# A Trainium2 decoder layer: column halves with query tiles 0,3 and 1,2, inverse sums as repeated stationaries, and separate semaphores for two reloads

## What is computed

```python
def one_block(args):            # a block of 128 queries
    q_blk, i = args
    s = jnp.einsum('bqhd,bkhd->bhqk', q_blk, k).astype(jnp.float32) * scale
    s = jnp.where(kpos[None, :] <= qpos[:, None], s, -jnp.inf)
    p = jax.nn.softmax(s, axis=-1).astype(v.dtype)
    return jnp.einsum('bhqk,bkhd->bqhd', p, v)
...
mix = jnp.concatenate([y_rwkv, y_mla], axis=-1) @ w_out[l]
x = layer_norm(ALPHA * x + mix, ln1_g[l], ln1_b[l])
f = jnp.square(jax.nn.relu(x @ w_ffn1[l])) @ w_ffn2[l]
x = layer_norm(ALPHA * x + f, ln2_g[l], ln2_b[l])
```

## Time and profile before

| | |
|---|---|
| time, median of 3 runs | 1356.23 us (1355.48 to 1357.2) |
| the profiled execution's own time | 1353.33 us |
| its span in the profile | 1351.5 us |
| granted TensorE clock, mean | 0.998 |
| busy of the span: PE, PEld | 97%, 79% |
| busy of the span: DVE, ACT, POOL | 70%, 35%, 37% |
| chain that ended last, PE's share | 49% |

### The profile page before, as it was taken

The page is one execution under the profiler, slowest core; times in us unless marked ns, Lnnn a source line. Parts: engine busy times, 40 slices in busy tenths (PEclk is TensorE's granted clock), DMA queues, the critical chain, the costliest instruction groups (busy, mean ns, idle before and its releaser), DMA issues.

```text
span 1351.5 us, 23894 instructions
## 1 busy us (share of the span) xinstructions
PE 1315.0 (97%) x9900; PEld 1071.2 (79%) x9900; DVE 945.5 (70%) x1110; ACT 474.8 (35%) x796; POOL 497.0 (37%) x323
## 2 busy tenths in 40 slices
PE   7999999999999989989999999999999999999997
PEld 6877677877776789986688878888888888888886
DVE  3657975257777634439677988877777787669877
ACT  3143643146555433334104522212222444333330
POOL 0000112001876210002084778766774354444030
PEclk9999999999999999999999999999999999999999
DMA  5111444779639952224222345444436986666562
GB/s 225 62 48 32 141 157 156 184 169 292 183 101 288 221 127 53 59 64 140 87 101 94 117 137 198 142 147 164 156 125 226 356 288 219 190 198 200 190 205 106
DMA packets 147372, 214.50 MB, mean 159 GB/s; under 512 B 79960, under 2 KB 86240, under 8 KB 146624
## 3 DMA queue, kind: packets, MB, share of 16 engines
q1 hardware_dynamic: 146976, 211.92, 49.3%
q10 hardware_dynamic: 288, 1.05, 0.2%
HBM read 137.89 MB, written 66.39 MB: 151 GB/s over the span
## 4 chain that ended last, share of the span: by engine, by line
PE 49%; DVE 3%; POOL 1%; issue 1%; ACT 1%; DVEq 0%; POOLq 0%; ACTq 0%
PE banks L2523 23%; PE banks L2410 18%; PE banks L2326 5%; PE banks L2398 2%; POOL tile_h L3083 1%; PE banks L2371 1%; DVE wout_lo L2736 0%; POOL tile_s L3083 0%; DVE y_all L2756 0%; DVE first_relu L2870 0%; PE banks L2352 0%; DVE gn_scale L2747 0%; PE banks L156 0%; PE banks L2337 0%; DVE yr_full L2762 0%
## 5 line engine op out<-in xcount | busy, mean ns | idle before, releaser
L2523 PE MATMUL banks<-stage_b_hi,stage_a_hi 128*128 128x512 f32 x448 | 174.3, 389 | 0.0
L2523 PE MATMUL banks<-stage_b_lo,stage_a_hi 128*128 128x512 f32 x448 | 174.3, 389 | 0.0
L2523 PE MATMUL banks<-stage_b_hi,stage_a_lo 128*128 128x512 f32 x448 | 174.3, 389 | 0.0
L2898 DVE TENSOR_TENSOR stage_a_lo<-stage_a_raw,stage_a_hi 128x1024 fp32r<-128x1024 f32 x56 | 97.7, 1745 | 35.2 <-ACT stage_a_hi L2665 35.2
L2665 ACT ACTIVATE stage_a_hi<-stage_a_raw 128x1024 fp32r<-128x1024 f32 x56 | 59.4, 1061 | 120.9 <-DMA stage_b_raw<-in_w_ffn 98.4
L2523 PEld LDWEIGHTS banks<-stage_b_lo,stage_a_hi 128*128 128x128 f32 x448 | 84.1, 188 | 17.6
L2523 PEld LDWEIGHTS banks<-stage_b_hi,stage_a_hi 128*128 128x128 f32 x448 | 84.1, 188 | 17.4
L2523 PEld LDWEIGHTS banks<-stage_b_hi,stage_a_lo 128*128 128x128 f32 x448 | 84.1, 188 | 17.3
L852 POOL TENSOR_TENSOR hT<-hT,rate 128x1024 f32<-128x1024 f32 x4 | 13.5, 3370 | 210.1 <-DVE kk_tile L773 210.1
L428 PE MATMUL banks<-xT_hi,win_hi 128*128 128x512 f32 x288 | 90.6, 396 | 0.0
L428 PE MATMUL banks<-xT_lo,win_hi 128*128 128x512 f32 x288 | 88.8, 389 | 0.0
(11 more groups left out here) (423 smaller groups left out, 3590.1 us busy)
## 6 DMA issues: line engine op xcount, KB each, us to landing
stage_b_raw<-in_w_ffn SPq DMA_DIRECT2D x50, 512.0 KB, 5.0
stage_a_raw<-hid_s SPq DMA_DIRECT2D x32, 512.0 KB, 4.0
w_landed<-in_w_ffn SPq DMA_DIRECT2D x30, 512.0 KB, 4.7
hid_s<-tile_s SPq DMA_DIRECT2D x60, 256.0 KB, 4.4
stage_a_raw<-hid_h SPq DMA_DIRECT2D x24, 512.0 KB, 4.0
hid_h<-tile_h SPq DMA_DIRECT2D x42, 256.0 KB, 2.0
win_raw<-in_w_in SPq DMA_DIRECT2D x20, 512.0 KB, 3.6
x_tok<-in_x SPq DMA_DIRECT2D x8, 512.0 KB, 7.6
```

The source lines that it names most:

```text
L2523: last = nc.tensor.matmul(ps[:, bank, :], s[a][:, j, tok], s[b][:, j, :], start=p == 0 and j == 0 and n == 0, stop=p == NP - 1 and j == 1 ...
L2898: V.tensor_tensor(s["a_lo"][:], s["a_raw"][:], s["a_hi"][:].bitcast(F32), ALU.subtract).then_inc(lo2, 1)
```

## The change

- `k.halves_of = ((0, 3), (1, 2))`: in each group, column half 0 takes the first and the last query tile, half 1 the two in the middle. As long as both of a half's tiles need a key tile, one matmul of 256 columns reads them with a stride; after that, one of 128 columns serves the farther tile.
- The inverse sums are no longer spread over a diagonal. Each column of inverse sums, repeated 64 times by its access pattern, is the stationary operand, and the identity is the moving one: four matmuls of 128 columns for each group in place of two of 256. DVE's two products with the identity are gone, with the wait before them; the addition of the two units' sums becomes a reduction (one input), and the reciprocal waits for the same group's inverse of the head before.
- `k.quarters` addresses two query tiles that aren't neighbours, so y leaves in pieces of 128 columns (512 bytes) in place of 256 (1 KB): eight DMAs of 64 KB for each head in place of four of 128 KB. `y_moved` counts 128 a head.
- `cum` and `beta` get semaphores of their own. ACT's first decays wait for `cum` alone. DVE waits for the three first reloads at the end of the stage, and SP for everything as before.

```diff
--- before.py
+++ after.py
@@ -878,7 +878,7 @@
     late_t = (mem.at("late_probs_t_03", 134, [P, 4, HALF]), mem.at("late_probs_t_45", 197, [P, 2, HALF]),
               mem.at("late_probs_t_67", 201, [P, 2, HALF // 2]))
     early_t = (mem.at("early_probs_t_01", 76, [P, 2, HALF]), mem.at("early_probs_t_23", 80, [P, 2, HALF // 2]))
-    inverse_diag = [mem.at(f"inverse_sums_diagonal{c}", kb, [P, 2, P]) for c, kb in enumerate((110, 190))]
+    inverse = mem.at("inverse_sums", 3.75, [P, TT])
     w_nope = (k.w_nope_raw, mem.at("w_nope_hi", 197, [P, QLT, NH, HD], F32R),
               mem.at("w_nope_lo", 106, [P, QLT, NH, HD], F32R))
     w_last = mem.at("w_nope_last_hi", 76, [P, QLT, 2, HD], F32R)
@@ -913,7 +913,6 @@
     tops = mem.at("row_max_parts", 3.25, [P, 2, TT])
     sums = mem.at("row_sums", 3.5, [P, 2, TT])
     total = mem.at("row_sums_added", 3.625, [P, 4])
-    inverse = mem.at("inverse_sums", 3.75, [P, TT])
     zeros = mem.at("zeros", 112, [P, HALF])
     dram = lambda name, shape: nc.dram_tensor(name, shape, F32, kind="Internal").ap()
     nope_d, rope_d, key_d = ([dram(f"{n}_d{j}", [NH * rows, S]) for j in range(2)]
@@ -926,7 +925,9 @@
     flat = lambda pair, rows=slice(0, P): ps[rows, pair[0]:pair[0] + 2, :].rearrange("p b n -> p (b n)")
     lo64, hi64, pe32, sw32 = slice(0, 64), slice(64, 128), slice(64, 96), slice(96, 128)
     halves = [slice(b * HALF, (b + 1) * HALF) for b in range(2)]
-    k.quarters = lambda x, rows, tile, c: x[rows, tile, :].rearrange("p (a c j) -> p a c j", a=2, c=2)[:, :, c, :]
+    k.halves_of = ((0, 3), (1, 2))
+    k.quarters = lambda x, rows, tile, c: x[rows, tile, :].rearrange("p (a t q) -> p a t q", a=2, t=4)\
+        [:, :, k.halves_of[c][0]:k.halves_of[c][1] + 1:k.halves_of[c][1] - k.halves_of[c][0], :]
 
     SOLVE_FROM = (SB - 2, 20, 15, 10, 0)
     LATE = {0: ("nope", 3), 1: ("key", 2), 3: ("key", 3)}
@@ -1008,7 +1009,8 @@
             "b_values_taken", "b_late_hi", "b_late_lo", "b_last_hi")
         stage_out = sems(nc, ctx, "b_stage_out0", "b_stage_out1")
         set_in = sems(nc, ctx, "b_set_in0", "b_set_in1", "b_set_in2")
-        bias_ready, first_exps, head0_in = sems(nc, ctx, "b_bias_ready", "b_first_exps", "b_head0_in")
+        bias_ready, first_exps, head0_in, cum_in = sems(nc, ctx, "b_bias_ready", "b_first_exps", "b_head0_in", "b_cum_in")
+        beta_in, = sems(nc, ctx, "b_beta_in")
         s_done, exp_done, t_done = sems(nc, ctx, "b_s_done", "b_exp_done", "b_t_done")
         evicted = sems(nc, ctx, "b_evicted_dve", "b_evicted_act")
         inverse_ready = sems(nc, ctx, "b_inverse_late", "b_inverse_early")
@@ -1095,8 +1097,10 @@
                         sp.dma_start(blocks(k.inv_d, c), solved[c][:]).then_inc(x_out, 16)
                 if h >= 5:
                     sp.wait_ge(s_done, NU * (h + 1))
-                    dst, src = ((k.cum_all, k.cum_d), (k.beta_all, k.beta_d))[h - 5]
-                    sp.dma_start(dst[:], src).then_inc(reloaded, 16)
+                    if h == 5:
+                        sp.dma_start(k.cum_all[:], k.cum_d).then_inc(cum_in, 16)
+                    else:
+                        sp.dma_start(k.beta_all[:], k.beta_d).then_inc(beta_in, 16)
                 if h == 6:
                     sp.wait_ge(x_out, 32 * NB)
                     sp.dma_start(k.first_v[:], k.v_d[:, :, 0:CH]).then_inc(first_in, 16)
@@ -1112,11 +1116,14 @@
                 sp.wait_ge(y_split, 4 * h + 4)
                 for c in range(2):
                     for dst, src in ((ym_hi, k.att_hi), (ym_lo, k.att_lo)):
-                        sp.dma_start(k.quarters(dst, rows, h // 2, c).bitcast(F32),
-                                     src[64 * c:64 * c + 64, :].rearrange("p (a j) -> p a j", a=2).bitcast(F32))\
-                            .then_inc(y_moved, 16)
-            sp.wait_ge(y_moved, 64 * (NH - 1))
-            sp.wait_ge(reloaded, 16 * 5)
+                        for a in range(2):
+                            part = src[64 * c:64 * c + 64, 2 * P * a:2 * P * (a + 1)].rearrange("p (t q) -> p t q", t=2)
+                            sp.dma_start(k.quarters(dst, rows, h // 2, c)[:, a, :, :].bitcast(F32), part.bitcast(F32))\
+                                .then_inc(y_moved, 16)
+            sp.wait_ge(y_moved, 128 * (NH - 1))
+            sp.wait_ge(reloaded, 16 * 3)
+            sp.wait_ge(cum_in, 16)
+            sp.wait_ge(beta_in, 16)
             sp.wait_ge(small_in, 16 * 5)
             sp.wait_ge(first_in, 16 * 7)
 
@@ -1237,28 +1244,35 @@
                         left(LATE[h])
                     else:
                         pe.wait_ge(y_read[g], h)
+                base = (4, 0)[g]
                 for kt in kts:
-                    for c in range(2):
-                        q0 = (4, 0)[g] + 2 * c
-                        if kt > q0 + 1:
-                            continue
-                        if g == LATER:
-                            src, at = ((late_t[0][:, kt, :], 4) if kt < 4 else (late_t[1][:, kt - 4, :], 4) if kt < 6
-                                       else (late_t[2][:, kt - 6, :], 6))
-                        else:
-                            src, at = (early_t[0][:, kt, :], 0) if kt < 2 else (early_t[1][:, kt - 2, :], 2)
-                        lo = max(kt, q0) * P
-                        last = mm(ps[64 * c:64 * c + 64, BANK_Y + g, lo - q0 * P:2 * P], v_all[:, kt, h, :],
-                                  src[:, lo - at * P:(q0 + 2 - at) * P], start=kt == 0, stop=kt == q0 + 1)
+                    if g == LATER:
+                        src, at = ((late_t[0][:, kt, :], 4) if kt < 4 else (late_t[1][:, kt - 4, :], 4) if kt < 6
+                                   else (late_t[2][:, kt - 6, :], 6))
+                    else:
+                        src, at = (early_t[0][:, kt, :], 0) if kt < 2 else (early_t[1][:, kt - 2, :], 2)
+                    for c, (near, far) in enumerate(k.halves_of):
+                        near, far = base + near - at, base + far - at
+                        out = ps[64 * c:64 * c + 64, BANK_Y + g, 0:2 * P]
+                        if kt <= near + at:
+                            last = mm(out.rearrange("p (t q) -> p t q", t=2), v_all[:, kt, h, :],
+                                      src.rearrange("p (t q) -> p t q", q=P)[:, near:far + 1:far - near, :],
+                                      start=kt == 0, stop=False)
+                        elif kt <= far + at:
+                            last = mm(out[:, P:2 * P], v_all[:, kt, h, :], src[:, far * P:(far + 1) * P],
+                                      start=False, stop=kt == far + at)
                 if kts[-1] == (7, 3)[g]:
                     last.then_inc(pv_done[g], 1)
 
             def inverse_out(h, g):
 
                 pe.wait_ge(inverse_ready[g], h + 1)
-                for c in range(2):
-                    last = mm(ps[64 * c:64 * c + 64, BANK_Y + g, 2 * P:4 * P], ones[:, 0:HD],
-                              inverse_diag[c][:].rearrange("p j q -> p (j q)"), start=True, stop=True)
+                of = (4, 0)[g]
+                for j in range(2):
+                    for c in range(2):
+                        last = mm(ps[64 * c:64 * c + 64, BANK_Y + g, (2 + j) * P:(3 + j) * P],
+                                  inverse[:, of + k.halves_of[c][j]:of + k.halves_of[c][j] + 1].to_broadcast([P, HD]),
+                                  ident[:], start=True, stop=True)
                 last.then_inc(y_done[g], 1)
 
             for name in FRONT[EARLY:11]:
@@ -1386,7 +1400,7 @@
                     if late_step(h, i - 1) is not None:
                         stage_late(h, late_step(h, i - 1))
                     if h == NH - 1 and i == 6:
-                        act.wait_ge(reloaded, 16 * 5)
+                        act.wait_ge(cum_in, 16)
                         act.wait_ge(x_out, 32 * NB)
                         A_(k.first_decay[:], k.cum_all[:, :, 0:CH], ACT.Exp, scale=-EXP_M05)
                         A_(k.first_undecay[:], k.cum_all[:, :, 0:CH], ACT.Exp, scale=EXP_M05).then_inc(first_exps, 1)
@@ -1462,18 +1476,12 @@
                 dve.wait_ge(exp_done, NU * h + (8, 12)[g])
                 row_sums = sums[:, 0, of]
                 if g == LATER:
-                    step.mark(V.tensor_tensor(total[:], sums[:, 0, of], sums[:, 1, of], ALU.add))
+                    step.mark(V.reduce_sum(total[:], sums[:, :, of].rearrange("p m q -> p q m"), AX_X))
                     step.wait()
                     row_sums = total[:]
-                step.mark(V.reciprocal(inverse[:, of], row_sums))
-                step.wait()
-                if h or g == EARLIER:
-                    dve.wait_ge(y_done[1 - g], h + g)
-                for c in range(2):
-                    pair = inverse[:, of][:, 2 * c:2 * c + 2].rearrange("p (j o) -> p j o", o=1).to_broadcast([P, 2, P])
-                    square = ident[:].rearrange("p (o q) -> p o q", o=1).to_broadcast([P, 2, P])
```

(10 more changed lines are left out.)

## The result

The changed kernel took 1360.5 us (median of 13 runs, 1356.8 to 1366.1) where the kernel before took 1355.4 on the same chip: ratio 1.0041, 95% interval 1.0027 to 1.0055. The likeliest case of the forecast, no change at 1356.7, did not come. The time lies inside the range, nearest to rival C (1360.6).

What follows compares the result with a forecast made beforehand. PE ends the attention stage, only 1.1 us behind SP's queue, so 1.3 of PE's 12.6 us come out; -1.3 + 1.8 for the cold clock = +0.5, on the 1356.23 median 1356.7 us, range 1347.5 to 1361.0.

Steps and rivals of the forecast that it cites:

- rival C: SP's queue from y(3) to y(6): every added issue is paid, block end +2.6, 1360.6 us; chance 0.16.
- Part one: PE's balanced column halves in the attention stage: 0.43 us saved per group, 6.9 us for eight heads.
- strict program order: PE's matmuls start and end in program order, so a group would save about 0.32 us instead of 0.43.
- Part two: Inverse sums as stationaries: 0 cost on PE, head 5's stall (2.3 us) and halved clock (1.65 us) gone.
- Part three, transfers: DMA work for each head's y in half-size pieces: 3.0 us, where it was 2.3.
- Part three, issues and landings: SP's queue: eight issues a head, 2.6 us more; y(5) lands 457.6, y(6) ready 462.0; stage gives 1.3 us.
- the prediction's own sign: Forecast is wrong if the next block starts before 466 or after 471, or PE stays busy to block's end.
- rivals A and B: A: issue cost follows bytes, 1352.1, chance 0.12. B: PE's end decides, 1343.6 or about 1347, chance 0.10.
- Part four: Own semaphores: ACT in head 7 waits some 3 us for cum, covered by SP, which ends later.
- What comes back: PE idles about 459 to 469 and starts the next block cold: 1.8 us lost, bounds 0 and 2.5.

Runs made afterwards that it cites:

- halves_only: Changed kernel with the inverse over the identity's diagonal as before, keeping new column halves, eight y copies and separate semaphores: 1358.2 us, ratio 1.0037.
- before_reload_early: Kernel before with the 2 MB reloads and their small tables issued one head earlier: 1351.8 us, ratio 0.9976.
- the second execution: Second profiled execution of the unedited changed kernel, on another chip: 1358.5 us.
- the first execution: First profiled execution of the changed kernel, the longest of its 13 runs: 1366.1 us.
- y_in_eight: Kernel before with each y copy cut in two, eight copies of 64 KB a head, still 1 KB pieces: 1360.3 us, ratio 1.0046.
- after_six: Changed kernel with six y copies a head in place of eight: 1355.6 us, ratio 1.0010.
- before_longer: Kernel before with 96 two-column matmuls added behind PE's last inverse of the stage: 1373.2 us, ratio 1.0138.
- kept_busy_less: Changed kernel with 64 and 54 unused identity transposes on PE behind head 7's late and early inverses: 1358.1 us, ratio 1.0030.
- six_reordered: Changed kernel with six y copies a head and SP's transfers after y(4) in another order: 1356.8 us, ratio 1.0014.
- after_reload_early: Changed kernel with the 2 MB reloads and their small tables issued one head earlier: 1357.4 us, ratio 1.0018.

## Where the prediction was right, and why it missed the time

- Part one was right: tail 1.67, early value products 1.23 from their start to the next transpose (445.72 to 446.95) where it was 1.66, and PE's timetable to 0.3 us at 438.19. Both groups gave 0.43, and neither the 0.32 of strict program order, for which the prediction shows no working.
- Part two was right: no cost on PE, no stall, no halved clock. That the reduction would escape POOL's hold was not tested: it ran at 417.91, before POOL's copies started at 419.02. halves_only and before_reload_early show that the stall is made by DVE's two-input operations meeting the copies.
- Part three, transfers: the term was too high and did no harm. I took 3.0 us of DMA work for a head's y, where it was 2.3, for pieces of half the size. Only one column half leaves in 512-byte pieces; the other's two tiles are neighbours and leave in 1 KB pieces, against what I wrote under the change. A packet of 512 bytes took 34 ns and one of 1 KB 66 to 71, so the work stayed at 2.2 us.
- Part three, issues and landings: right in the second execution, mis-sized in the first. I took eight issues of y(4) as 6.6 us; they took 6.6 in the second execution and 7.7 in the first, where three pairs were held. In the first execution cum took 15.7 and not 11.6, and y(5), which I had landing at 457.6, landed at 463.0. POOL waited for that landing, y(6) came 5.5 us later than forecast, and the block ended 4.3 us later than before instead of 1.3 sooner. The failed term is the landing of y(5), 5.4 us too early; 1.7 of it is the later first store, and part of the rest are the last parts that came alone. y_in_eight (+0.46%) and after_six (0.3% less than the change) show that the number of issues costs time in the block. They don't say how much of the change's own 0.41% it is, for its second execution has the block's end at 470.1 and is slow all the same.
- Rival C, to which I gave 0.16, had y(6) at 465.9 and the block 2.6 later. The first execution went further (467.5 and 4.3), the second not at all (462.6 and -0.6). By the prediction's own sign, a next block that starts after 471, the first execution with 475.2 refutes the forecast and the second with 470.3 doesn't. That the median of 1360.5 meets its 1360.6, and that the time stayed inside the range, is luck in part: C has nothing of the 3 to 7 us of the chunk stage but 1.8 of clock.
- Part three, rivals A and B fell. An issue of 64 KB held SP for 0.6 us as one of 128 KB does, against A. Against B, neither the earlier reloads nor the new order let PE's end decide.
- Part four was right in kind: ACT waits for cum, 7.5 and 1.9 us where I had 3, and is covered by SP both times (PE's end 465.6 against 474.9, 458.0 against 470.1). No kernel with ACT waiting for beta was run beside the new order of PE's work.
- "What comes back" had the clock right (2.0 us against 1.8) and missed a term. In the eight profiled executions with the new column halves the chunk stage took 121.3 to 126.5 us, in the five with the old ones (before_longer apart) 116.8 to 120.4. Part is the cold clock, but kept_busy_less with a whole clock at its start took 124.1. The rest are waits of PE for its own instructions, 0.3 to 3.4 us each, and the halved clock at the long ones near 20 us into the stage. The waits from 12 us into the stage to its end, of 0.25 us and more, sum to 3.4 us in before and 7.4 in the first execution of the change; in the second they sum to 4.5. The large one near 20 us is not all: from 60 to 115 us into the stage the first execution falls another 6.7 us behind before, the second 1.9. I took the next block's work as given once its start was fixed; that was the step that failed for the second execution.

What stays open: why the instruction packets come later in the changed kernel. The length of PE's program alone doesn't say it: after_six and six_reordered have stops of 0.7 and 1.0 with the changed PE program, and their chunk stages still took 122.0 and 123.9, of which the cold clock is some 2.5. The "rest" behind the chunk stage ran from 760.6 to 767.5 us over all kernels without relation to the edits, so a single profile can't carry a difference of 3 us there. In y_in_eight, after_reload_early and the second execution of the change part of that is a stop of 2.0 to 3.3 us that stands across SP's mark, so that the chunk stage looks shorter by 1.0 to 1.7 us and the rest longer.

## What to carry to other kernels

Savings on an engine that is last by 1.1 us are worth 1.1 us, and less if they are paid for with issues in the queue that is second: count the issues between the last free moment of that queue and the stage's end, and give an issue behind large transfers a range for being held, not 0.65 us. Follow the last copy to its landing, for the next step waits for that and not for the issue. When a busy engine is made to wait, look at the next stage as well as at the wait. When a chain says "issue", look at the instruction queue among the DMA queues. The better change here was not to make the work smaller but to move one group of transfers (0.9976, 0.9966 to 0.9986); by the rows, two engines' operations then no longer meet and the last copy lands sooner, and how much each is worth was not separated.

## What the runs showed that I had not expected

- DVE's addition of two 128x4 sums took 3.65 us beside POOL's copies and 0.15 to 0.48 otherwise; shifting POOL by 5 us removes the same stall as rewriting DVE's work.
- Halving a copy halves its transfer, not its issue: 0.61 us for 128 KB and for 64 KB; a 16 KB table behind 6 MB of reloads held SP for up to 9.8 us.
- PE stopped for up to 3.4 us in the middle of a run of equal matmuls and went on 1.2 to 1.65 us after a 16 KB packet of the instruction queue had landed; the granted clock was 0.50 for 3.4 us at the stops of 1.8 to 3.4 us near 20 us into the stage.
